# Gate matrices of a product-key expert layer: two FP32 passes replaced by one split FP32R product of 256 columns

## The reference, cut to what matters

```
cidx = si[:, :, 0, :, None] * N_KEYS + si[:, :, 1, None, :]
top_s, sel = lax.top_k(cand.reshape(C, PEER_HEADS, K * K), K)
eidx = jnp.take_along_axis(cidx.reshape(...), sel, axis=-1)
g = jax.nn.softmax(top_s, axis=-1)
u = u_tab[eidx]
act = jax.nn.gelu(jnp.einsum('chkd,cd->chk', u, xb), approximate=False)
w = (g * act)
return jnp.einsum('chk,chkd->cd', w, v_tab[eidx])
```

## Time and profile before

| | us |
|---|---|
| three runs | 1763.35, 1765.33, 1772.0 |
| median | 1765.33 |
| span of the profiled execution | 1774.7 |
| gate stage in it | 1158 to 1392 |
| PE busy | 1710.5 (96%) |
| DVE, ACT, POOL busy | 1044.9, 826.9, 900.8 |

### The profile page before, as it was taken

How to read it: one execution, slowest core, us unless ns; L and a number is a source line. 1 busy time by engine, 2 the same in 40 slices (tenths; PEclk the granted TensorE clock), 3 DMA queues, 4 the chain that set the end, 5 groups by cost and what they waited for, 6 DMA issues and landing times. The chain is left out here.

```text
span 1774.7 us, 34933 instructions
## 1 busy us (share of the span) xinstructions
PE 1710.5 (96%) x12583; PEld 1606.4 (91%) x12583; DVE 1044.9 (59%) x2198; ACT 826.9 (47%) x1147; POOL 900.8 (51%) x275
## 2 busy tenths in 40 slices
PE   8899799999999999999998999999999999999997
PEld 8889799999997999999678999999999978888886
DVE  7857654345344554344885891745555377777776
ACT  4578343334547433345435544644444443333332
POOL 4676468887682378876205588776666500000000
PEclk9999999999998999999988999999999999999999
DMA  5443335555452245554202466665555687777774
GB/s 212 143 144 118 113 126 190 190 188 192 143 190 72 72 167 190 188 183 160 93 1 84 164 234 236 210 205 177 178 177 177 216 266 240 240 241 243 239 242 160
DMA packets 77453, 310.79 MB, mean 175 GB/s; under 512 B 8768, under 2 KB 10304, under 8 KB 60736
## 3 DMA queue, kind: packets, MB, share of 16 engines
q1 hardware_dynamic: 75024, 306.14, 51.3%
q10 hardware_dynamic: 2352, 3.59, 0.6%
HBM read 290.82 MB, written 18.87 MB: 175 GB/s over the span
## 5 line engine op out<-in xcount | busy, mean ns | idle before, releaser
L759 POOL TENSOR_TENSOR lo<-raw,hi 128x2048 fp32r<-128x2048 f32 x127 | 584.3, 4610 | 378.1 <-ACT hi L584 306.0
L362 PE MATMUL ps<-xc,hi 128*128 128x256 f32 x1912 | 544.3, 285 | 5.7 <-DVE ps L2052 3.3
L363 PE MATMUL ps<-xcl,hi 128*128 128x256 f32 x1912 | 536.3, 280 | 0.0
L364 PE MATMUL ps<-xc,lo 128*128 128x256 f32 x1912 | 536.1, 280 | 0.0
L362 PEld LDWEIGHTS ps<-xc,hi 128*128 128x128 f32 x1912 | 362.6, 190 | 8.6 <-issue 6.9
L798 POOL TENSOR_TENSOR lo<-raw,hi 128x1024 fp32r<-128x1024 f32 x128 | 304.7, 2404 | 128.8 <-ACT hi L1767 128.7
L363 PEld LDWEIGHTS ps<-xcl,hi 128*128 128x128 f32 x1912 | 364.3, 191 | 0.1
L1767 ACT ACTIVATE hi<-raw 128x1024 fp32r<-128x1024 f32 x256 | 264.9, 1058 | 211.3 <-PE ps L364 199.0
L364 PEld LDWEIGHTS ps<-xc,lo 128*128 128x128 f32 x1912 | 360.6, 189 | 0.0
L2472 DVE TENSOR_TENSOR lo<-raw,hi 128x1024 fp32r<-128x1024 f32 x128 | 156.4, 1222 | 81.1 <-ACT hi L1767 81.0
L362 PE MATMUL ps<-hi,wgh 128*128 128x512 f32 x512 | 199.4, 389 | 1.8 <-DVE wgl L2483 1.8
(11 more groups left out here) (497 smaller groups left out, 3426.6 us busy)
## 6 DMA issues: line engine op xcount, KB each, us to landing
raw<-in_w_u SPq DMA_DIRECT2D x128, 512.0 KB, 4.3
raw<-in_w_v SPq DMA_DIRECT2D x128, 512.0 KB, 4.2
raw<-in_w_up SPq DMA_DIRECT2D x44, 1024.0 KB, 4.8
raw<-in_w_down SPq DMA_DIRECT2D x22, 1024.0 KB, 4.7
raw<-in_w_fox SPq DMA_DIRECT2D x16, 1024.0 KB, 5.0
act_save<-act_out SPq DMA_DIRECT2D x64, 256.0 KB, 2.1
act_in<-act_save SPq DMA_DIRECT2D x64, 256.0 KB, 3.2
raw<-in_w_xbc SPq DMA_DIRECT2D x12, 1024.0 KB, 5.0
```

The costliest lines, as they stand in the source:

```text
L362: pe.matmul(o, ah, bh, start=start, stop=False)
L363: pe.matmul(o, ah, bl, start=False, stop=False)
L364: return pe.matmul(o, al, bh, start=False, stop=stop)
L759: return g.tensor_tensor(lo[slot][:], raw[slot][:], hi[slot][:].bitcast(F32), ALU.subtract)
```

## The change

The gates of a token become one FP32R matmul of 256 columns. The gate is split into a rounded part and a remainder (`gate_lo`). `oj` now has two halves: the one-hot times the rounded gate, and the one-hot times the remainder. A group's four products fill two banks, so there are two buffers in place of four. In each group:

- DVE makes the column one-hot, adds the low half of the group before last to `gates` (`add_gates`), multiplies the one-hot by the rounded gate, makes the row one-hot, and multiplies the one-hot by the remainder for two of the four tokens.
- ACT multiplies by the remainder for the other two tokens (`low_gates`) and copies the high half to `gates` (`copy_gates`).
- ACT's turn in the gate stage has a new order (`gate_turn`): copy, first split, low product, copy, Gelu, second split, low product.
- The two buffers `act_out` become one, so Gelu waits for the store of the pair before it. SP's order is unchanged.

Besides, some tiles move in SBUF (not shown).

```diff
...
+    act_out = sb("act_out", [P, 2, SEQ])
     hot_at = place["at"]
-    oi = [sb(f"oi{i}", [P, GT, P]) for i in range(2)]
-    oj = [sb(f"oj{i}", [P, GT, P]) for i in range(2)]
+    oj = [sb(f"oj{i}", [P, 2, GT, P], F32R) for i in range(2)]
+    oi = [sb(f"oi{i}", [P, GT, P], F32R) for i in range(2)]
...
+    def gate_half(b, part):
+        return ps[:, 4 + 2 * b:6 + 2 * b, :].rearrange("p q (t h j) -> p j (q t) h", t=2, h=2)[:, :, :, part]
...
-        def store_act(m, s):
+        def store_act(m):
             sp.wait_ge(a_gelu, m + 1)
             dst = act_save[m] if isinstance(m, int) else act_save[bass.ds(m, 1)].rearrange("o p n -> (o p) n")
-            sp.dma_start(dst, act_out[s][:].rearrange("p a b -> p (a b)")).then_inc(act_stored[s], 16)
+            sp.dma_start(dst, act_out[:].rearrange("p a b -> p (a b)")).then_inc(act_stored, 16)
...
             def gate_products(n, b):
-                pe.wait_ge(row_hot, n + 1)
-                pe.wait_ge(col_gates, n + 1)
-                if not isinstance(n, int) or n >= 4:
-                    pe.wait_ge(g_evac, n - 3)
+                pe.wait_ge(picks_made, n * 4 + 4)
+                pe.wait_ge(col_low, n + 1)
+                if not isinstance(n, int) or n >= 2:
+                    pe.wait_ge(g_evac, n - 1)
                 else:
-                    pe.wait_ge(ht_evac, n + 1)
+                    pe.wait_ge(ht_evac, 2 * n + 2)
                 for t in range(GT):
-                    m = pe.matmul(ps[:, 4 + b, t * P:(t + 1) * P], oi[b % 2][:, t, :], oj[b % 2][:, t, :], start=True, stop=True)
+                    o = ps[:, 4 + 2 * b + t // 2, (t % 2) * 2 * P:(t % 2 + 1) * 2 * P]
+                    m = pe.matmul(o.rearrange("p (a b) -> p a b", a=2), oi[b][:, t, :], oj[b][:, :, t, :], start=True, stop=True)
                 m.then_inc(g_mm, 1)
...
                 for b in range(4):
                     u_half(i * 2 + b // 2, b // 2, b % 2)
-                    gate_products(i * 4 + (b - 2 * GATES_AT), b)
+                    gate_products(i * 4 + (b - 2 * GATES_AT), b % 2)
...
-            def gelu(m, s, stores):
+            def gelu(m, s):
                 act.wait_ge(e_used, m * 2 + 2)
-                if stores is not None:
-                    act.wait_ge(act_stored[s], stores)
-                nc.scalar.activation(act_out[s][:].rearrange("p a b -> p (a b)"), ps[:, s, :], ACT.Gelu).then_inc(a_gelu, 1)
-
-            def take_gates(n, b):
+                if not isinstance(m, int) or m >= 1:
+                    act.wait_ge(act_stored, m * 16)
+                nc.scalar.activation(act_out[:].rearrange("p a b -> p (a b)"), ps[:, s, :], ACT.Gelu).then_inc(a_gelu, 1)
+
+            def low_gates(n, b):
+                act.wait_ge(picks_made, n * 4 + 2)
+                for t in range(2):
+                    place = oj[b][:, 1, t, :]
+                    ins = nc.scalar.activation(place, place.bitcast(F32), ACT.Copy, scale=gate_lo[:, bass.ds(n * GT + t, 1)])
+                ins.then_inc(col_low, 1)
+
+            def copy_gates(n, b):
                 act.wait_ge(g_mm, n + 1)
-                nc.scalar.activation(gates[:, :, bass.ds(n * GT, GT)],
-                                     ps[:, 4 + b, :].rearrange("p (t j) -> p j t", t=GT), ACT.Copy).then_inc(g_evac, 1)
+                nc.scalar.activation(gates[:, :, bass.ds(n * GT, GT)], gate_half(b, 0), ACT.Copy).then_inc(g_copied, 1)
...
             act.wait_ge(lst_mm, 1)
             act.wait_ge(h_saved, 16)
-            with nc.scalar.Fori(GATES_AT // 2, GATES_END // 2) as i:
-                u_turn(i, 0, True)
-                u_turn(i, 1, True)
+            low_gates(0, 0)
+            low_gates(1, 1)
+
+            def gate_turn(i, s, following):
+                g = i * 4 + (2 * s - 2 * GATES_AT)
+                copy_gates(g, 0)
+                split(i * 2 + (2 + s), s, 0, i * 16 + 32, True)
+                if following:
+                    low_gates(g + 2, 0)
+                copy_gates(g + 1, 1)
+                gelu(i * 2 + s, s)
+                split(i * 2 + (2 + s), s, 1, i * 16 + 32, True)
+                if following:
+                    low_gates(g + 3, 1)
+
+            with nc.scalar.Fori(GATES_AT // 2, GATES_END // 2 - 1) as i:
+                gate_turn(i, 0, True)
+                gate_turn(i, 1, True)
+            gate_turn(GATES_END // 2 - 1, 0, True)
+            gate_turn(GATES_END // 2 - 1, 1, False)
             with nc.scalar.Fori(GATES_END // 2, PAIRS // 2) as i:
...
-            def one_hots(n, b):
+            gate_list = ps[:, 3, 0:SEQ]
+            rounded = oj[0][:, 0, 0:2, :].rearrange("p a b -> p (a b)")
+            ch(v.tensor_copy(rounded, gate_list))
+            ch(v.tensor_tensor(gate_lo[:], gate_list, rounded.bitcast(F32), ALU.subtract))
+
+            def picks(n, b, earlier):
 
                 def hot(place, w):
                     number = ps[:, 2, bass.ds(n * GT + w * SEQ, GT)].unsqueeze(2).broadcast_to([P, GT, P])
-                    return v.tensor_tensor(place[b][:], iota[:].unsqueeze(1).broadcast_to([P, GT, P]), number, ALU.is_equal)
+                    return v.tensor_tensor(place, iota[:].unsqueeze(1).broadcast_to([P, GT, P]), number, ALU.is_equal)
 
                 if not isinstance(n, int) or n >= 2:
                     v.wait_ge(g_mm, n - 1)
-                hot(oj, 1).then_inc(col_hot, 1)
-                hot(oi, 0).then_inc(row_hot, 1)
+                hot(oj[b][:, 1], 1).then_inc(picks_made, 1)
+                if earlier:
+                    add_gates(n - 2, b)
                 gate = ps[:, 3, bass.ds(n * GT, GT)].unsqueeze(2).broadcast_to([P, GT, P])
-                v.wait_ge(col_hot, n + 1)
-                v.tensor_tensor(oj[b][:], oj[b][:], gate, ALU.mult).then_inc(col_gates, 1)
-
-            one_hots(0, 0)
-            one_hots(1, 1)
+                v.wait_ge(picks_made, n * 4 + 1)
+                v.tensor_tensor(oj[b][:, 0], oj[b][:, 1].bitcast(F32), gate, ALU.mult).then_inc(picks_made, 1)
+                hot(oi[b][:], 0).then_inc(picks_made, 1)
+                low = oj[b][:, 1, 2:GT, :]
+                rest = gate_lo[:, bass.ds(n * GT + 2, 2)].unsqueeze(2).broadcast_to([P, 2, P])
+                v.wait_ge(picks_made, n * 4 + 2)
+                v.tensor_tensor(low, low.bitcast(F32), rest, ALU.mult).then_inc(picks_made, 1)
+
+            def add_gates(n, b):
+                v.wait_ge(g_copied, n + 1)
+                place = gates[:, :, bass.ds(n * GT, GT)]
+                v.tensor_tensor(place, place, gate_half(b, 1), ALU.add).then_inc(g_evac, 1)
+
+            picks(0, 0, False)
+            picks(1, 1, False)
             with nc.vector.Fori(1, GROUPS_OF_TOKENS // 2) as i:
-                one_hots(i * 2, 0)
-                one_hots(i * 2 + 1, 1)
+                picks(i * 2, 0, True)
+                picks(i * 2 + 1, 1, True)
+            add_gates(GROUPS_OF_TOKENS - 2, 0)
+            add_gates(GROUPS_OF_TOKENS - 1, 1)
```

More of the change, by code:

```diff
@@ L152, in build @@
     ident = sb("ident", [P, P])
+    stat = sb("stat", [P, 128])
+    gate_lo = sb("gate_lo", [P, SEQ], at=base)
     iota = sb("iota", [P, P])
-    stat = sb("stat", [P, 128])
     to(128)
@@ L161, in build @@
         lo.append(sb(f"lo{s}", [P, UNIT], F32R))
-    rs = sb("rs", [P, 3, 32])
     to(64)
@@ L191, in build @@
     rows = sb("rows", [P, NROWS])
+    rs = sb("rs", [P, 3, 32])
     to(64)
@@ L294, in build @@
     sif_sel = [sb(f"sel{i}", [P, NT, PH, TOPK], at=xn_at + 8192 + 1024 * i) for i in range(2)]
[L296 to L299, removed]
+    place["at"] = xh_at + 2 * KC * SEQ * 4
+    act_out = sb("act_out", [P, 2, SEQ])
     hot_at = place["at"]
-    oi = [sb(f"oi{i}", [P, GT, P]) for i in range(2)]
-    oj = [sb(f"oj{i}", [P, GT, P]) for i in range(2)]
+    oj = [sb(f"oj{i}", [P, 2, GT, P], F32R) for i in range(2)]
+    oi = [sb(f"oi{i}", [P, GT, P], F32R) for i in range(2)]
     gates_at = place["at"]
@@ L305, in build @@
     assert place["at"] <= nc.sbuf_usable_end, (place["at"], nc.sbuf_usable_end)
-    act_in = [sb(f"act_in{i}", [P, 2, SEQ], at=hot_at + 2048 * i) for i in range(2)]
-    wgh = [sb(f"wgh{i}", [P, 2, SEQ], F32R, at=(hot_at + 4096, xh_at + 64)[i]) for i in range(2)]
-    wgl = [sb(f"wgl{i}", [P, 2, SEQ], F32R, at=(hot_at + 6144, xh_at + 64 + 2048)[i]) for i in range(2)]
+    place["at"] = hot_at
+    to(128)
+    v_at = place["at"]
+    act_in = [sb(f"act_in{i}", [P, 2, SEQ], at=v_at + 2048 * i) for i in range(2)]
+    wgh = [sb(f"wgh{i}", [P, 2, SEQ], F32R, at=(v_at + 4096, xh_at + 64)[i]) for i in range(2)]
+    wgl = [sb(f"wgl{i}", [P, 2, SEQ], F32R, at=(v_at + 6144, xh_at + 64 + 2048)[i]) for i in range(2)]
     hf = sb("hf", [P, NT, D], at=gates_at)
@@ L324, in build @@
     e_hi_done, u_lo_done, v_lo_done, e_used = sem("e_hi_done"), sem("u_lo_done"), sem("v_lo_done"), sem("e_used")
-    act_stored = [sem(f"act_stored{i}") for i in range(2)]
+    act_stored = sem("act_stored")
     act_loaded = [sem(f"act_loaded{i}") for i in range(2)]
```

(58 more changed lines are left out.)

6 lines of the change are left out of this document (3 added, 3 removed).

## The result

The changed kernel is slower: 1777.5 us against 1768.8 us (medians of 14 runs each), a ratio of 1.0071 with a 95% interval of 1.0046 to 1.0097. The forecast was 1777 us and 0.7%. It was built on a median of 1765.3 from three runs, so that the absolute time comes out within a microsecond is in part luck; the size to compare is the difference.

A forecast was written before the change was run, and what follows sets the result against it. PE bounds the gate stage now; after the change a ring through ACT and the loads would: 5.70 + 0.95 + 0.60 + 0.49 = 7.74 us a pair against 7.37, 1765.3 + 11.8 = 1777 us, range 1763 to 1797.

The forecast's parts named there:

- The gain on offer: PE in the gate stage: a group's product falls from 0.89 to 0.47 us, so PE alone needs 6.53 us a pair.
- The ring: Gate stage: Gelu, store, load of m+3, first split, low product, copy, next Gelu take 7.74 us a pair; 7.37 now.
- The size: Gate stage, 32 pairs at 0.37 us more each: +11.8 us, between -7 and +25.
- the last pairs catch up: End of the gate stage: PE's spare time lets the last pair end early against ACT, under 1 us, not counted.
- DVE's own work: DVE in the gate stage: 2.7 us a group, 5.4 us a pair, which hides in the 7.74 us.
- its upper bound of 1.2: DVE's addition to gates in runs of four: from 0.60 up to 1.2 us, which would make 6.6 us a pair.
- The contention: DVE's low product, with two SBUF operands, can wait up to 2.4 us for POOL's remainders in the gate stage.
- a rival at 0.19 with a price of 8.2: DVE held up by POOL bounds the gate stage: 8.2 us a pair, +27 us, 1792 us; chance 0.19.
- One buffer for Gelu's output: ACT in the gate stage: Gelu waits for the store ahead of it, costed at nothing.
- The signs: Gate-stage profile: Gelu to Gelu 7.7 us, splits wait 1 to 3 us for loads every pair, PE at 85%.

The follow-up runs named there:

- both: The changed kernel with Gelu ahead of the first split and the remainder for DVE's low product in accumulator memory: 6.61 us a pair, ratio 0.9868.
- low_psum: The changed kernel with the remainder also written to accumulator memory, from where DVE's low product reads it: 7.66 us a pair, ratio 1.0073.
- loads_first: The changed kernel with SP's order alone changed, loads of pair m+3 issued ahead of the store of pair m: 7.30 us a pair, ratio 1.0022.
- gelu_early: The changed kernel with Gelu moved ahead of the first split in ACT's gate turn: 7.38 us a pair, ratio 1.0026.
- gelu_mid: The changed kernel with Gelu moved up two places in ACT's gate turn, directly behind the first split: 6.82 us a pair, ratio 0.9937.
- before_ring: The kernel before with ACT's gate turn alone reordered to first split, both copies of gates, Gelu, second split: 7.73 us a pair, ratio 1.0055.

## Why the prediction was right, point by point

- **The gain on offer.** 0.47 us for a group's product was forecast, 0.48 measured. PE alone at 6.53 us a pair: "both" gives 6.61 with PE full. Most of the 0.08 us is the step of the u matmuls, 0.1178 us in that stretch of "both" and 0.1159 on average in the kernel before (the last section).
- **The ring.** Forecast 5.70 + 0.95 + 0.60 + 0.49 = 7.74 us; measured 5.76 + 0.96 + 0.59 + 0.48 = 7.79 us. It was opened at Gelu, opened at the load, shortened by 1.07 us, lengthened by 0.58 us, and built into the kernel before. In each case the pair moved as the sum says, until the next limit.
- **The size.** Forecast 32 x 0.37 = 11.8 us. The profile has 15.2 us from pair 27 to pair 59, and 1.7 us less behind it, so 13.5 us. 28 x 0.44 = 12.2 are the steady pairs; the first three turns, not costed, take 24.0 us against 21.4. That the last pairs catch up was put at under 1 us and left out. The medians differ by 8.7 us, the ratio makes it 12.6 us, and its interval is 8 to 17 us of 1768.8.
- **DVE's own work.** Forecast 5.4 us a pair at a step of 0.60; the addition in runs of four took 0.67 to 0.69 us like the others, so its upper bound of 1.2 was not needed.
- **The contention.** The text had "One such wait a pair makes 5.4 + 2.4 = 7.8 on DVE, about the ring; it is not added to it", and made the rest a rival at 0.19 with a price of 8.2. The count was right: one of the two low products of each pair waits. That it is not added to the ring fits low_psum, which takes it away and is as slow as the change. As a limit of its own it was put too high: with the ring open a pair takes 7.30 to 7.38 us (loads_first, gelu_early), the pace of the kernel before, since the wait adds 1.5 to 1.9 us and not 2.4. So the change had two faults, and the ring, the longer of the two, hides the other. Opening the ring alone brought no gain over the kernel before, and taking away the contention alone brought none; the ring made shorter (gelu_mid) also moved the contention, to 6.82 us, and brought 0.6%. The prediction did not say how far the pair would fall once its ring was gone. The rule of the Trainium skill ("SBUF — State Buffer", "Who interferes with whom") holds in the low products of these profiles: with one operand in accumulator memory, all 64 products took 0.41 us. The product that waits ends 0.28 us behind POOL's listed end, though it takes 0.41 alone; the listed spans of POOL are rough.
- **One buffer for Gelu's output** was costed at nothing, and the change's waits from 1158 to 1398 us hold none of ACT for a store.
- **The signs.** Gelu follows Gelu by 7.79 us (7.7 named), a split waits 2.2 us for its load (70.9 / 32; 1 to 3 named), and ACT waited 70.9 us for loads against 17.4 for DVE. PE fell to 89% (218.8 of 245 us), not 85%.

## What to carry to other kernels

Where engines work through queues in a fixed order, follow each wait until it comes back to its own engine, and divide the length of that ring by the number of rounds that it spans: a move of one instruction from behind a wait to ahead of it can turn a ring over two rounds into a ring over one. Look for such a ring above all where a store and the next load share a queue. And after finding the limit, ask how far below it the next one lies; here two repairs each looked useless until both were made, and the pace that the second limit allowed (7.38 or 6.82 us a pair) hung on where one instruction stood.

## What the runs showed of the hardware that was not expected

The step of the u and feed-forward matmuls, from one start to the next, comes in two sizes at the same granted clock. In the stretch from 300 to 400 us, the same feed-forward stage in both, the kernel before issued 851 matmuls:

```profile
300.00:400.00 100.00, 100.00 (x851) 100.00 (x850) 41.72 (x84) 38.23 (x30) 81.11 (x19) 1.00 0.53 188
```

and the change 885:

```profile
300.00:400.00 100.00, 100.00 (x885) 100.00 (x884) 42.70 (x86) 38.29 (x30) 84.97 (x19) 1.00 0.54 191
```

0.1175 and 0.113 us each, at a granted clock of 1.00 in both. It does not go with the change: loads_first has 851, gelu_early and "both" have 885. In the u products ahead of the gate stage a pair takes 5.65 us in the kernel before and in low_psum, 5.44 us in the change and in before_ring, whatever the step in the feed-forward stage of the same run. So the step changes within an execution: low_psum has the short one in the feed-forward stage and the long one in the u products. Over a pair of 48 u matmuls it makes 0.2 us, which matters to a pair's time only where PE sets the pace. Gelu of pair 0 starts at 1001.0 us in the kernel before and at 983.7 us in the change, though the work ahead of it is the same; how much of that is the step was not taken apart. It is why the spans of the two profiles could not be compared here. What sets the step stays open.
